# Norm weights folded in by diagonal products, one product for the expert slots, the overflow slots worked out during the gather, output units split earlier, and a fifth place for raw weights

## The reference, cut to what matters

```
h = rmsnorm_2(x, norm_ffn_g)                    # x / rms(x) * g, g one weight per channel
group_logits  = h @ rg_w + rg_b                 # 4 groups
expert_logits = h @ re_w + re_b                 # 32 experts, 8 in a group
grp = argmax(group_logits); top-2 inside the group; gate = p_grp * softmax(top_val)
for each expert: y = (silu(h_e @ w_gate) * (h_e @ w_up)) @ w_down      # 1024x512, 1024x512, 512x1024
x = x + sum of the two gated y of the token
out = rmsnorm_2(x, final_norm_g)
```

## Time and profile before

| | |
|---|---|
| Time before, three runs | 2052.15 us median (2045.65 to 2056.08) |
| The profiled execution, its own time | 2047.25 us |
| Its span | 2045.4 us |
| Busy: PE, weight loads, DVE, ACT, POOL | 1786.2, 1355.8, 1187.0, 912.7, 198.7 us |
| Chain that ended last | PE 66%, DVE 18%, ACT 11%, issue 2%, DMA 2% |
| Stretch 1280 to 1340 (out2) | PE busy 49.80 of 60 us, clock 0.87 |
| Stretch 1340 to 1400 (route, start of moe) | PE busy 24.89 of 60 us, clock 0.59 |
| Stretch 1680 to 1740 (expert loop) | PE busy 56.78 of 60 us, clock 1.00 |

### The profile page before, as it was taken

The page is one execution under the profiler, slowest core; times in us unless marked ns, Lnnn a source line. Parts: engine busy times, 40 slices in busy tenths (PEclk is TensorE's granted clock), DMA queues, the critical chain, the costliest instruction groups (busy, mean ns, idle before and its releaser), DMA issues.

```text
span 2045.4 us, 19323 instructions
## 1 busy us (share of the span) xinstructions
PE 1786.2 (87%) x7882; PEld 1355.8 (66%) x7882; DVE 1187.0 (58%) x1368; ACT 912.7 (45%) x1046; POOL 198.7 (10%) x174
## 2 busy tenths in 40 slices
PE   5599998788797999999999998857999999999992
PEld 4375765444485787787778766646777777777771
DVE  3513443655525343433349783357888888888884
ACT  4321443544323231313253203235777777777772
POOL 0000000555000000000000030030101111101100
PEclk7799999899997999999999997858999999999996
DMA  6202444000221222222122100125899999899983
GB/s 244 114 21 103 160 190 153 1 1 0 82 83 42 103 83 103 82 99 87 42 83 83 62 21 21 57 104 209 330 351 348 354 346 343 334 346 341 353 334 133
DMA packets 54813, 324.40 MB, mean 159 GB/s; under 512 B 12609, under 2 KB 13121, under 8 KB 17986
## 3 DMA queue, kind: packets, MB, share of 16 engines
q1 hardware_dynamic: 42624, 306.86, 40.3%
q0 software_dynamic: 9216, 8.42, 1.3%
q10 hardware_dynamic: 2882, 7.85, 1.1%
HBM read 327.27 MB, written 20.97 MB: 170 GB/s over the span
## 4 chain that ended last, share of the span: by engine, by line
PE 66%; DVE 18%; ACT 11%; issue 2%; DMA 2%; POOL 0%; PEldq 0%; SPq 0%; POOLq 0%; DVEq 0%; ACTq 0%
PE ps L496 33%; PE ps L1181 9%; DVE wlo L1744 8%; PE ps L1154 5%; ACT whi L1232 5%; PE ps L1049 2%; PE ps L753 2%; DVE ac L1821 2%; PE ps L556 2%; ACT yb L1266 2%; PE ps L1140 1%; PE ps L647 1%; PE ps L598 1%; PE ps L894 1%; PE ps L1163 1%
## 5 line engine op out<-in xcount | busy, mean ns | idle before, releaser
L1744 DVE TENSOR_TENSOR wlo<-raw,whi 128x2048 fp32r<-128x2048 f32 x284 | 646.2, 2287 | 286.8 <-ACT whi L1232 286.0
L1232 ACT ACTIVATE whi<-raw 128x2048 fp32r<-128x2048 f32 x284 | 538.8, 1913 | 253.2 <-PE ps L496 127.3
L496 PE MATMUL ps<-hH,whi 128*128 128x512 f32 x624 | 251.4, 403 | 20.8 <-issue 12.0
L496 PE MATMUL ps<-hH,wlo 128*128 128x512 f32 x624 | 248.5, 398 | 0.0
L496 PE MATMUL ps<-hL,whi 128*128 128x512 f32 x624 | 248.5, 398 | 0.0
L1154 PE MATMUL ps<-whi,xH 128*128 128x512 f32 x512 | 205.7, 402 | 0.0
L1154 PE MATMUL ps<-whi,xL 128*128 128x512 f32 x512 | 202.1, 395 | 0.0
L1154 PE MATMUL ps<-wlo,xH 128*128 128x512 f32 x512 | 200.3, 391 | 0.0
L496 PEld LDWEIGHTS ps<-hH,whi 128*128 128x128 f32 x624 | 118.5, 190 | 51.4 <-issue 14.0
L496 PEld LDWEIGHTS ps<-hL,whi 128*128 128x128 f32 x624 | 118.7, 190 | 28.7 <-issue 0.5
L496 PEld LDWEIGHTS ps<-hH,wlo 128*128 128x128 f32 x624 | 118.4, 190 | 29.1
(11 more groups left out here) (424 smaller groups left out, 2701.5 us busy)
## 6 DMA issues: line engine op xcount, KB each, us to landing
raw<-in_experts SPq DMA_DIRECT2D x192, 1024.0 KB, 7.0
raw<-in_streamed SPq DMA_DIRECT2D x93, 1024.0 KB, 4.8
xT<-in_x SPq DMA_DIRECT2D x1, 2048.0 KB, 13.4
h_scratch<-hN ACTq DMA_DIRECT2D x4, 512.0 KB, 2.6
Y<-y_scratch SPq DMA_DIRECT2D x4, 512.0 KB, 8.5
Y<-y_scratch ACTq DMA_DIRECT2D x4, 512.0 KB, 8.9
out<-xN SPq DMA_DIRECT2D x4, 512.0 KB, 2.6
ctxT<-in_ctx SPq DMA_DIRECT2D x1, 1024.0 KB, 17.2
```

The costliest lines, as they stand in the source:

```text
L496: ins = e.matmul(o, l, r, start=(i == 0), stop=(i == len(prs) - 1))
L1232: e.activation(u.hi, u.raw, ACT.Copy).then_inc(*p.inc("hi", n, on="hi"))
L1744: e.tensor_tensor(u.lo, u.raw, u.hi.bitcast(F32), ALU.subtract).then_inc(*p.inc("lo", n, on="lo"))
```

## The change

Six edits:

- **Diagonal products.** ACT makes gdiag, 8 matrices of 128 x 128 with the norm's weights on the diagonal. Behind each block of out2 PE multiplies the block of xT with its gdiag (`gained`, four float32 products of 128 columns), which transposes and weights in one, and ACT copies this to hN. The multiplication on POOL and the load of `grow` are gone. ACT then scales hN in place by rcol and issues the store of each quarter right behind it, before the two conversions. The plain transposes (`token_major`, needed for xN at the very end) move behind the norm's sums: 0 to 2 at once, 3 behind "pos", 4 to 7 behind the first table. The copies of them on ACT follow its two conversions.
- **One product for the slots.** R1 and the weighted one-hots are rounded (fp32r), and "tt" and "ty" are one product of 64 columns ("tab 0"), and 16 for the overflow ("tab 1").
- **Overflow during the gather.** The overflow block on DVE follows the first `numbers`, ahead of the wait for the gathered tokens, and "tab 1" on PE stands ahead of `turn_x(0)`.
- **Output units split early.** ACT and DVE convert U_OUT2[2] at m = 2, U_OUT2[3] at m = 4 and the first expert unit at m = 6. In the sums of the norm, the last logits go behind the last sum instead of ahead of it.
- **A fifth raw place**, at `PH + 8192`, first used for u(2) 0. Its first load waits for the gates (gk) and dd, whose neighbours lie there.
- **In the loop**, DVE's `use` of u(x) 1 moves behind the two multiplications of the activation.

```diff
     for x in range(1, NEXP):
+        if x == 2:
+            raw_ring.append(Place(PH + 8192))
         U_E["g", x] = expert_units("g", x)
...
+        def gained(m):
+            b = ps.take(("gN", m), ("act", "gN", m))
+            if m == 0:
+                p.wait_ge(*done("act", "gd", 7))
+            p.wait_ge(*done(*b.before))
+            for i in range(4):
+                ins = e.matmul(b.t[:, i * 128:(i + 1) * 128], xT[:, m, i * 128:(i + 1) * 128], gdiag[:, m, :], start=True,
+                               stop=True)
+            ins.then_inc(*p.inc("gN", m))
...
             if m:
                 logits(m - 1)
-                token_major(m - 1)
+                gained(m - 1)
...
-        logits(7)
         p.wait_ge(*done("act", "sq", 12, 7))
...
-        token_major(7)
-        p.also("mid")
+        logits(7)
+        gained(7)
+        for m in range(3):
+            token_major(m)
...
-        table(("tt", 0), 32, Ot)
-        table(("ty", 0), 32, Oy)
+        token_major(3)
+        table(0, 64, Oty)
+        for m in range(4, 8):
+            token_major(m)
+        table(1, 16, Rty)
...
         half_mm(0, "g", 0)
         half_mm(0, "g", 1)
-        table(("tt", 1), 7, Rt[:, :, 0:7])
-        table(("ty", 1), 7, Ry[:, :, 0:7])
...
+        for m in range(8):
+            e.activation(gdiag[:, m, :], ident, ACT.Copy, scale=col("norm_ffn_g_2", m)).then_inc(*p.inc("gd", m))
...
         for m in range(8):
+            if m == 2:
+                convert(U_OUT2[2])
             if m == 4:
-                convert(U_OUT2[2])
+                convert(U_OUT2[3])
             if m == 6:
-                convert(U_OUT2[3])
-            if m == 7:
                 convert(U_E["g", 0][0])
...
         for i in range(4):
-            e.activation(hN[:, i, :], xN[:, i, :], ACT.Copy, scale=rcol[:, i:i + 1]).then_inc(*p.inc("hN", i))
+            e.activation(hN[:, i, :], hN[:, i, :], ACT.Copy, scale=rcol[:, i:i + 1]).then_inc(*p.inc("hN", i))
+            p.wait_ge(*done("act", "hN", i))
+            e.dma_start(hd_[i * 128:(i + 1) * 128, :], hN[:, i, :]).then_inc(*p.land("hd", "hd", i))
         convert(U_E["g", 0][1])
         convert(U_E["u", 0][0])
-        for i in range(4):
-            p.wait_ge(*done("pool", "hN", i))
-            e.dma_start(hd_[i * 128:(i + 1) * 128, :], hN[:, i, :]).then_inc(*p.land("hd", "hd", i))
+        for m in range(8):
+            token_major(m)
...
-        overflow_places()
         gates()
         for x in range(NEXP):
             r = x % 2
-            for n in U_E["u", x]:
-                use(n)
+            use(U_E["u", x][0])
             p.wait_ge(*done("act", "sig", x))
             TT(ac[r], ac[r], ps["eg", x].t[:, :], ALU.mult, "g", x)
             p.wait_ge(*done("dve", "g", x))
             p.wait_ge(*done("pe", "use", U_E["u", x][1]))
             TT(ac[r], ac[r], ps["eu", x].t[:, :], ALU.mult, "u", x)
+            use(U_E["u", x][1])
...
-        p.wait_ge(*done("dma", "grow"))
-        for i in range(4):
-            p.wait_ge(*done("act", "hN", i))
-            e.tensor_tensor(hN[:, i, :], hN[:, i, :], grow, ALU.mult).then_inc(*p.inc("hN", i))
...
+            if n == FIFTH:
+                p.wait_ge(*done("dve", "gk"))
+                p.wait_ge(*done("act", "dd"))
```

More of the change, by code:

```diff
@@ L391, in build @@
     U_E["d", NEXP - 1] = expert_units("d", NEXP - 1)
-    AFTER = {U_E["u", 0][0]: (("pe", "den", 3),), U_E["g", 1][1]: (("pool", "hN", 3),)}
+    FIFTH = min(u.n for u in units if u.place == PH + 8192)
+    AFTER = {U_E["u", 0][0]: (("pe", "den", 3),), U_E["g", 1][1]: (("pe", "gN", 7),)}
     ctxT = at("ctxT", PH + 6144, [8, 256])
@@ L441, in build @@
     fgb = at("fgb", PH + 11264, [1024])
-    grow, R1 = at("grow", PH + 12288, [1024]), at("R1", PH + 11264, [8, 128])
+    gdiag, R1 = at("gdiag", PH + 12288, [8, 128]), at("R1", PH + 11264, [8, 128], FR)
     xN, hN = at("xN", PH, [4, 1024]), at("hN", PH + 4096, [4, 1024])
@@ L1119, in pe_program, with table @@
         ins.then_inc(*p.inc("pos"))
-        def table(name, n, vals):
-            b = ps.take(name, ("dve",) + name)
-            p.wait_ge(*done("dve", "R", name[1]))
+        def table(k, n, vals):
+            b = ps.take(("tab", k), ("dve", "ty", k))
+            p.wait_ge(*done("dve", "R", k))
             p.wait_ge(*done(*b.before))
@@ L2342, in numbers @@
             e.scalar_tensor_tensor(out=tv[:, 1, 0:n], in0=t, scalar=-1.0, in1=tv[:, 0, 0:n], op0=ALU.add,
[L2343 removed]
+                                   op1=ALU.add).then_inc(*p.inc(name, k))
             p.wait_ge(*p.own())
[L2345 to L2347 removed]
+            copy(dst[:, o:o + n], tv[:, 1, 0:n], p.inc("id" + name, k))
+        numbers("tt", 0, ps["tab", 0].t[:, 0:32], 0, idt)
@@ L2348, in dve_program @@
         convert(U_E["g", 0][1])
-        numbers(("ty", 0), 32, 0, idy)
-        def overflow_places():
-            TS(nov, cnt, 128.5, None, ALU.is_gt)
-            TS(q12, p12, 127.5, None, ALU.is_gt)
-            for lim in (256.5, 384.5):
-                p.wait_ge(*p.own())
-                TS(oi, cnt, lim, None, ALU.is_gt)
-                TS(u12, p12, lim - 1.0, None, ALU.is_gt)
-                p.wait_ge(*p.own())
-                TT(nov, nov, oi, ALU.add)
-                TT(q12, q12, u12, ALU.add)
+        numbers("ty", 0, ps["tab", 0].t[:, 32:64], 0, idy)
@@ L2398, in overflow_places @@
-            copy(ovi[:, :], ovf[0:1, :], p.inc("ovi"))
-            numbers(("tt", 1), 7, 32, idt)
-            numbers(("ty", 1), 7, 32, idy)
+            TT(nov, nov, oi, ALU.add)
+            TT(q12, q12, u12, ALU.add)
+        p.wait_ge(*p.own())
+        p.wait_ge(*done("pool", "z32"))
+        e.tensor_tensor_scan(oi, nov, z32[:, :], 0.0, ALU.add, ALU.add).then_inc(*p.inc())
+        e.scalar_tensor_tensor(out=p12, in0=q12, scalar=-128.0, in1=p12, op0=ALU.mult, op1=ALU.add).then_inc(*p.inc())
@@ new lines, in dve_program @@
+        TS(u12, q12, 0.5, None, ALU.is_gt)
+        p.wait_ge(*p.own())
+        TT(ob, oi, nov, ALU.subtract)
+        TT(R1, b8(iot, 128), p12.unsqueeze(2).broadcast_to([P, 8, 128]), ALU.is_equal)
+        p.wait_ge(*p.own())
+        for k in range(2):
+            TT(e8[:, k], rowb(ob, 32), O12[:, k], ALU.mult)
+        p.wait_ge(*p.own())
+        e.tensor_reduce(b12, e8.rearrange("p k i c -> p (k i) c"), AX.X, ALU.add).then_inc(*p.inc())
+        p.wait_ge(*p.own())
+        TT(b12, b12, q12, ALU.add)
@@ new lines, in dve_program @@
+        TT(ovt, b8(ob), j8, ALU.is_le)
+        TT(ovm, b8(oi), j8, ALU.is_gt)
+        p.wait_ge(*p.own())
+        TT(ovt, ovt, ovm, ALU.mult)
+        p.wait_ge(*p.own())
+        TT(ovt, ovt, b8(iota), ALU.mult)
+        p.wait_ge(*p.own())
+        e.tensor_reduce(ovf[:, 0:8], ovt, AX.X, ALU.add).then_inc(*p.inc())
+        copy(ovf[:, 8:16], oi[:, 31:32].broadcast_to([P, 8]), p.inc())
+        p.wait_ge(*p.own())
+        copy(ovi[:, :], ovf[0:1, :], p.inc("ovi"))
+        numbers("tt", 1, ps["tab", 1].t[:, 0:7], 32, idt)
@@ L2402, in gates @@
+        numbers("ty", 1, ps["tab", 1].t[:, 8:15], 32, idy)
         def gates():
```

102 lines of the change are left out of this document (40 added, 62 removed).

## The result

| | before | after |
|---|---|---|
| Time, median of four runs each | 2049.26 us (2045.65 to 2056.08) | 2000.78 us (2000.16 to 2001.48) |
| Ratio, 95% interval | | 0.976 (0.9731 to 0.9789) |
| Profiled execution, span | 2045.4 us | 1998.8 us |

The expert loop of the changed kernel, the stretch from 1680 to 1740 us. The columns are the stretch, its length, PE, PEld, DVE, ACT and POOL busy, granted clock, DMA share, GB/s (against the earlier trace rows: PE 56.78, share 0.93).

The account below looks back on a forecast made before the run. PE was busy 87% of the span; losses lay in out2, route to moe, and a ring of waits in the expert loop. Gains 21.0 + 16.7 + 13.9 = 51.6 us gave 1995.65 us profiled, 1997 us forecast, range 1985 to 2012.

Parts of the forecast that it names:

- Early split: Out2: earlier weight conversions remove two PE stalls (4.81 and 4.90 us) and the slow clock behind each; 13.3 us gained.
- Diagonal products: Out2: four 128-column products replacing transposes cost 0.5 us more per block, seven ahead of the last sum; 3.5 us lost.
- The end of the stage: End of out2: block 7's logits go behind the sums and its plain transposes behind everything; 1.5 us gained.
- POOL's multiplication: Route: with it gone, DVE's four additions return from 9.24 to about 0.6 us; 8.6 us gained.
- first table: Slot table after route: one rounded product takes 1.8 to 2 us instead of 3.62; 1.6 us gained.
- Overflow during the gather: Before g(0): DVE's overflow work just fits into its wait for the gathered tokens; 0.5 us lost (0 to 3).
- g(0) to d(0): First expert: u(0) follows g(0) at once, and the stretch falls from 37.56 to 20.9 us; 16.7 us gained.
- The loop: Experts: PE's wait moves from `turn_a` to d(x), 1.07 to about 0.6 us; period 19.13 to 18.68; 13.9 us gained.
- The fifth place: Expert loop: gives a raw-weight transfer 3.1 us more, but gains nothing by itself.
- Rival 2: Expert loop: PE becomes the bound if aL comes in time, period 18.06 us, total 1976 us; chance 0.06.
- The last row of the table: Stretch from d(31) to the end: no gain predicted (0 us).
- the first row: Stretch from the start to PE's last wait for hL, before the output product runs freely: no gain predicted (0 us).

Follow-up runs that it names:

- undo_split: Changed kernel with the three early weight conversions of out2 put back to blocks 4, 6 and 7; 2010.24 us.
- add_first: Changed kernel with DVE adding block m ahead of the early conversion, at m = 2, 4, 6, in the output product's loop; 2000.13 us.
- al_first: Changed kernel with DVE making aL ahead of its third conversion of the expert loop, not behind it; 1969.19 us, ratio to before 0.9613.
- best: Changed kernel with the edits of al_first and add_first together; 1967.93 us, ratio to before 0.9608.
- pool_mults: Changed kernel with four idle 128x1024 multiplications on POOL where those of the norm's weights were; 2007.47 us.
- tables_float32: Changed kernel with one-hots and ranks of the slot tables (R1, Oty, Rty) in float32 again, still one product for both tables; 2006.55 us.
- four_places: Changed kernel without the fifth raw place; 2007.77 us.
- overflow_back: Changed kernel with DVE's overflow block back behind the conversions for g(0), and its table on PE back between g(0) and u(0); 2006.21 us.

## Why the prediction came out as it did

The time of 2000.78 us lies 4 us above the forecast and inside its range, and none of the rivals happened. Step by step:

- *Early split* ("Both stalls go ... Sum 13.3 us"): right that both go; undo_split brings both back. The step that failed stood in one sentence: "PE wants that block only after block 3". PE wants block 2's PSUM bank sooner, for the diagonal products that the same change puts in, and so waits 1.79 us, with slow products behind it (some seven 0.43 us apart, from 1292.67 to 1295.65). I had checked who reads the addition's output, not who reuses its bank. add_first prices it at 3.6 us (2.7 between al_first and best, where the clock at the end of the stage differed), about all that this stretch fell short by (11.3 - 8.5 = 2.8). Without the new stall the term would have held: undo_split against add_first is 62.90 - 48.77 = 14.1 us.
- *Diagonal products* (0.5 us a block): right, 0.50, so 3.5 us in all. *The end of the stage* (1.5 us): 1.5 in undo_split, whose stretch up to L is 62.90 - 60.87 = 2.0 us longer than before (3.5 - 1.5). In the changed kernel the slow last logits (1.78 us against 1.06) take some 0.7 of it back, which no step of the prediction had.
- *POOL's multiplication* and the *first table* (8.6 + 1.6): 10.5 measured against 10.2. The cause of the 9.24 us is shown by pool_mults.
- *Overflow during the gather* (-0.5): +0.1, hidden as the prediction said, though only just: table and gather end within 0.1 us of each other, and tables_float32 shows that what is added there is paid (1.6 us).
- *g(0) to d(0)*: 20.2 us where 20.9 was predicted. I had not divided the gain; it is 10.1 for the place of the overflow block, 5.1 for its table, 1.9 for the loop's order.
- *The loop*: the mechanism is right to the row (aL, 0.67 us, d(x) 8.67 us behind s, where 8.66 was predicted). The term was mis-sized, 9.65 instead of 13.9 us, for two reasons, and it is the larger part of the 5 us that the sum was too high. "What follows is unchanged" was not so: a wait ahead of d(x) costs its first products 0.34 us apart instead of 0.23, and d(x) to the next s took 10.12 instead of 10.01 us, so the period fell by 0.33, not 0.45. And there are 30 full periods, not 31: d(30) to d(31) is 14.84 us before and 14.95 after.
- *The fifth place* (nothing): nearly right at this period; four_places shows that most of the waits that it removes were covered, and 1.9 us were not. So 1.9 of the loop's 9.65 us are the fifth place's, which had been given none. It pays more (13 us) once the loop is faster.
- *Rival 2* (PE bound, 1976) gave PE alone 18.06 us. al_first shows that PE alone needs 17.83: to take a wait of 1.07 off the period of 19.13 is not enough, some 0.2 us more go with it (19.12 - 17.83 = 1.29). The reason is how an idle time is counted. In the changed kernel d(x) starts 1715.80 - 1714.73 = 1.07 us after the product ahead of it, where al_first has 0.23: 0.84 us lost, of which the profile lists 0.67, since it counts from the end of that product, 0.40 us after its start, and a product otherwise starts before that end (0.23 us behind the one ahead of it). With the 0.11 of the first product's distance this is 0.95 of the 0.96 us between the two kernels.
- The last row of the table: 0.6 us longer at the end, where the gathered Y lands; the same stretch took 39.9 us in pool_mults and 41.1 in add_first, so it is spread between runs. The 1.1 us in the first row is no gain of the change either, but luck: of the 46.6 us, 46.1 stand in the stretches that the change touches, against the 51.6 predicted. What makes the stretch ahead of the output product differ by up to 7 us was not settled; part of it is the landing of wqb, for which PE waited until 351.73 us in the changed kernel and 354.48 in four_places.

## What to carry to other kernels

When work is moved ahead of an addition that empties a PSUM bank, ask who takes that bank next, not only who reads the sum. When a wait moves instead of going, follow the ring once more: here exchanging two rows on one engine took away the new wait and gave 28.9 us over 30 periods (30 x 0.96), where the wait as listed (0.67) promised 20. And an edit that shows little by itself, as the fifth buffer (1.9 us), can be what lets the next one pay (13 us).

## What was not expected of the hardware

- A POOL multiplication with SBUF inputs holds up DVE operations with two SBUF inputs, and a TENSOR_SCALAR, each for about the length of one POOL instruction (1.61 to 1.84 us instead of 0.17), but not a TENSOR_REDUCE; a memset held up only the TENSOR_SCALAR (0.92 us).
- It may go the other way too. POOL's third gather instruction took 1.91 us beside DVE's overflow block (where R<-slots,p, with two SBUF inputs, ran for 1.22 us from 1348.61), and 0.99 where that block was moved away (overflow_back) and in the kernel before, with no cost in any. That this row of DVE held it up is not shown. The two rows, of the changed kernel and of overflow_back:

```profile
1348.78 1.91 POOL L2576 DMA_INDIRECT xg<-h_scratch,idt  x1 [0.30 <-issue]
```

```profile
1346.52 0.99 POOL L2578 DMA_INDIRECT xg<-h_scratch,idt  x1 [0.30 <-issue]
```

- PE's granted clock went to about half twice in the changed kernel's output product: behind a wait of 1.79 us, and at 1330 without any wait, behind eight float32 products of a single column; in overflow_back and al_first the same rows at the end ran at the full clock.
- The DMA engines carry 364 GB/s at a share of 0.98 without PE waiting. The Trainium skill, "Perfetto Trace Analysis", section "Roofline", gives 358 GB/s as a core's share when both cores of a pair read, and more for one alone; the rate here agrees.
